# Moving a sum of x from VectorE to GpSimd, with a new order for a pair's weights, taps, a gate and W_out's forms

## What is computed

```
hn   = rms_norm(x) * norm_g
h, b, c, z, a, g, zb = split(hn @ w_in)           # 1024 -> 7 x 512
out_a = b * conv3(c * h) * silu(z)
out_b = silu(layer_norm(conv31(a * sigmoid(g)) + bias)) * silu(zb)
y    = rms_norm(x + concat(out_a, out_b) @ w_out) * final_norm_g
```

## Time and profile before

| what | value |
|---|---|
| median of 3 runs | 1524.84 us (1523.97 to 1525.23) |
| the profiled execution's own time | 1527.43 us |
| its span | 1525.6 us |
| TensorE busy | 1506.6 us, 99% |
| VectorE busy | 1325.2 us, 87% |
| GpSimd busy | 658.0 us, 43% |
| ScalarE busy | 588.8 us, 39% |

### The profile page before, as it was taken

How to read it: one execution, slowest core, us unless ns; L and a number is a source line. 1 busy time by engine, 2 the same in 40 slices (tenths; PEclk the granted TensorE clock), 3 DMA queues, 4 the chain that set the end, 5 groups by cost and what they waited for, 6 DMA issues and landing times.

```text
span 1525.6 us, 19727 instructions
## 1 busy us (share of the span) xinstructions
PE 1506.6 (99%) x7114; PEld 1326.9 (87%) x7114; DVE 1325.2 (87%) x1339; ACT 588.8 (39%) x981; POOL 658.0 (43%) x569
## 2 busy tenths in 40 slices
PE   9999999999999999999999999999999999999998
PEld 8889999988888888888888888888888778888886
DVE  7899999999998899879899894798799788888875
ACT  7543342433342343333253322224444344444433
POOL 4777869312423341243432241116654444444441
PEclk9999999999999999999999999999999999999999
DMA  6798787789998889899878977766877754555541
GB/s 248 291 352 322 278 309 264 273 295 333 313 325 268 271 274 352 299 327 290 276 251 281 314 244 233 240 221 204 243 223 222 257 179 170 177 191 180 179 152 69
DMA packets 119416, 388.75 MB, mean 255 GB/s; under 512 B 17804, under 2 KB 23052, under 8 KB 115736
## 3 DMA queue, kind: packets, MB, share of 16 engines
q1 hardware_dynamic: 116776, 387.36, 74.8%
q10 hardware_dynamic: 2544, 0.14, 0.1%
HBM read 278.98 MB, written 108.47 MB: 254 GB/s over the span
## 4 chain that ended last, share of the span: by engine, by line
PE 92%; DVE 5%; issue 1%; DMA 1%; POOL 1%; ACT 0%; POOLq 0%; DVEq 0%; ACTq 0%
PE ps L2344 30%; PE ps L2346 30%; PE ps L2345 30%; DVE ps L2085 1%; PE ps L2466 0%; DMA outa_spill<-sets 0%; PE ps L2459 0%; DVE xf L1923 0%; PE ps L2479 0%; DMA conv_b<-conv_spill 0%; DVE conv_a_acc L2029 0%; PE ps L2550 0%; PE ps L2554 0%; DVE conv_b L2125 0%; DVE w_ring L1895 0%
## 5 line engine op out<-in xcount | busy, mean ns | idle before, releaser
L2085 DVE SCALAR_TENSOR_TENSOR ps<-v,conv_b_taps,ps 128x920 f32<-128x920 f32 (+2 forms) x580 | 630.6, 1087 | 17.4
L2344 PE MATMUL ps<-xf,w_ring 128*128 128x460 f32 (+1 forms) x1624 | 603.9, 372 | 4.2 <-ACT sets L1564 2.6
L2346 PE MATMUL ps<-xf,w_ring 128*128 128x460 f32 (+1 forms) x1624 | 603.3, 371 | 0.0
L2345 PE MATMUL ps<-xf,w_ring 128*128 128x460 f32 (+1 forms) x1624 | 601.5, 370 | 0.0
L2344 PEld LDWEIGHTS ps<-xf,w_ring 128*128 128x128 f32 x1624 | 305.8, 188 | 39.4 <-ACT sets L1564 3.7
L2345 PEld LDWEIGHTS ps<-xf,w_ring 128*128 128x128 f32 x1624 | 305.8, 188 | 34.0
L2346 PEld LDWEIGHTS ps<-xf,w_ring 128*128 128x128 f32 x1624 | 305.3, 188 | 34.3
L1564 ACT ACTIVATE sets<-ps 128x460 f32<-128x460 f32 x168 | 92.6, 552 | 476.7 <-PE ps L2346 457.2
L1323 POOL TENSOR_TENSOR w_ring<-w_ring_f,w_ring 128x512 fp32r<-128x512 f32 x28 | 39.8, 1422 | 217.1 <-ACT w_ring L1594 217.1
L2344 PE MATMUL ps<-out_forms,w_ring 128*128 128x512 f32 x288 | 114.6, 398 | 2.5 <-DVE h_rows_odd L2273 2.0
L2346 PE MATMUL ps<-out_forms,w_ring 128*128 128x512 f32 x288 | 112.9, 392 | 0.0
(11 more groups left out here) (231 smaller groups left out, 2137.6 us busy)
## 6 DMA issues: line engine op xcount, KB each, us to landing
w_ring<-weight_forms SPq DMA_DIRECT2D x294, 512.0 KB, 5.4
weight_forms<-xf SPq DMA_DIRECT2D x7, 2048.0 KB, 11.5
weight_forms<-w_ring SPq DMA_DIRECT2D x7, 2048.0 KB, 10.4
out_weight_forms<-w_ring SPq DMA_DIRECT2D x28, 512.0 KB, 6.7
w_ring_f<-in_w_in SPq DMA_DIRECT2D x56, 256.0 KB, 3.6
x_raw<-in_xT SPq DMA_DIRECT2D x31, 460.0 KB, 7.0
xf_f<-in_w_in SPq DMA_DIRECT2D x24, 512.0 KB, 6.9
x_row<-in_x_prompt SPq DMA_DIRECT2D x24, 512.0 KB
```

What stands on the lines that cost most here:

```text
L2085: dve.scalar_tensor_tensor(dst, window, wb[:, j, k:k + 1], part, ALU.mult, ALU.add).then_inc(taps_done, 1)
L2344: pe.matmul(out, ahi, bhi, start=(start and x == 0), stop=False, skip_group_check=goes_on)
L2345: pe.matmul(out, ahi, blo, start=False, stop=False, skip_group_check=goes_on)
L2346: mm = pe.matmul(out, alo, bhi, start=False, stop=(stop and x == len(terms) - 1), skip_group_check=goes_on)
```

## The change

`FORM_START = II + 5` begins W_out's forms in n = 19 instead of 15. `tap_quota` gives n = 2 and 3 four and six taps instead of eight and nine, and twelve instead of eleven to periods g = 5 and 9 of units 1 to 3. Pair 3's raw weights are loaded, copied and split earlier: on SyncE before `store_sums(1)`, on ScalarE before pair 0's second gate, on VectorE inside pair 0's work; for it GpSimd does `weight_sums(2)` before `sums_low(1)`. At a unit's beginning `gate_a` of the pair before comes ahead of P4's low half. And step 3 of the sums of x goes from VectorE to GpSimd, as the first instruction of the unit's first period.

```diff
 def tap_quota(n):
...
+    if n < 4:
+        return 4 if n == 2 else 6
...
-    return 11 if u < 4 else 12
+    return (12 if g in (5, 9) else 11) if u < 4 else 12
...
+FORM_START = II + 5
...
-    e, j = divmod(n - II - 1, FORM_PERIODS)
+    e, j = divmod(n - FORM_START, FORM_PERIODS)
...
             store_weights(1)
+            load_w(3)
             store_sums(1)
...
-                if n + 2 < II:
+                if 3 < n + 2 < II:
                     load_w(n + 2)
...
+            def last_form_sum(w):
+
+                pool.wait_ge(xf_sum, 4 * (w - 1) + 3)
+                pool.wait_ge(xf_lo, 7 * (w - 1) + P2 + 1)
+                pool.tensor_tensor(st[:, 1, :, :], st[:, 1, :, :], st[:, 0, :, :], ALU.subtract).then_inc(xf_sum, 1)
...
+            weight_sums(2)
             sums_low(1)
-            weight_sums(2)
...
             for n in range(II, III):
+                if n % G14 == 0:
+                    last_form_sum(unit(n))
                 if n > II:
                     last_quarter(n - 1)
...
             weight_high(2, 3)
+            weight_high(3, 0)
+            weight_high(3, 1)
             evacuate(0, 2)
...
-                else:
+                elif n > 2:
                     weight_high(n + 1, 0)
                     weight_high(n + 1, 1)
...
-                else:
-                    dve.wait_ge(xf_lo, 7 * (w - 1) + P2 + 1)
-                    dve.tensor_tensor(st[:, 1, :, :], st[:, 1, :, :], st[:, 0, :, :],
-                                      ALU.subtract).then_inc(xf_sum, 1)
...
                         scale_tile(1, 3)
+                        weights_low(3)
                     first_tile_made(n, "B")
...
-                if n < II - 1:
+                if 2 < n < II - 1:
                     weights_low(n + 1)
...
                     form_low(unit(n), P7)
-                    form_sum(unit(n), 3)
                     form_low(unit(n), P3)
+                    finish(n - 1)
                     form_low(unit(n), P4)
-                    finish(n - 1)
```

More of the change, by code:

```diff
@@ L1910, in form_sum @@
                                       ALU.subtract).then_inc(xf_sum, 1)
-                elif step == 2:
+                else:
                     dve.wait_ge(xf_lo, 7 * (w - 1) + P1 + 1)
                     dve.tensor_tensor(st[:, 0, :, :], st[:, 2, :, :], st[:, 0, :, :], ALU.add).then_inc(xf_sum, 1)
-                else:
-                    dve.wait_ge(xf_lo, 7 * (w - 1) + P2 + 1)
-                    dve.tensor_tensor(st[:, 1, :, :], st[:, 1, :, :], st[:, 0, :, :],
-                                      ALU.subtract).then_inc(xf_sum, 1)
             def form_low(w, i):
```

## The result

The changed kernel takes 1532.41 us (median of 8 executions, 1530.84 to 1534.53); the kernel before, run beside it, 1524.86. The ratio is 1.0045, 95% interval 1.0031 to 1.0059: slower by 7 us (7.5 by the medians), as predicted (1532.8). The profiled execution took 1534.53 us, its span 1532.7; the span before was 1525.6.

A forecast was written before the change was run, and what follows sets the result against it. TensorE, busy 99% of the span, was taken as the bound, with VectorE able to be late at units' beginnings. Units' beginnings +9.3 and unit 0 -1.3 gave +8.0 us on 1524.84: 1532.8 us, range 1518 to 1536.

The forecast's parts named there:

- GpSimd's long sum: Units' first periods: P4's sum as one 1840-column GpSimd instruction takes 4.1 us and holds VectorE's low half; net +9.3 us.
- The rival without a hold: Units' beginnings: GpSimd's long sum does not hold VectorE up and the 5.2 us go; 1518.3 us, chance 0.20.
- The order by turns: Units' beginnings: VectorE and GpSimd instructions of SBUF operands alternate, each for its whole length; the waiting one is next.
- the rival at 1523.4: Units' beginnings: sum holds VectorE, but form step and last quarters slip behind P4's low half; pair 3's weights in time; chance 0.15.
- VectorE instructions which read PSUM are not touched: Units' beginnings: VectorE work reading PSUM runs beside GpSimd unhindered; a GpSimd step takes 1.19 us beside it.
- the heading: "P4's sum on GpSimd", units' beginnings: moving the sum off VectorE makes low halves late; losses 14.5 us, net +9.3.
- Waits at the units' beginnings: TensorE late: unit 1 P3 0.25, P4 1.8 us; unit 2 P4 3.0; unit 3 P7 0.6, P3 0.7, P4 3.0.
- Slow stretches: Units 1 to 3: 1.7 us more lost to a slower clock behind each late P4.
- The 5.2 us now lost: Units 2 and 3: present losses of 0.7, 0.96, 1.9 and 1.7 us go, as gate_a is earlier and spills have landed.
- Unit 0: Pair 3's earlier weights and seven taps fewer bring `v` 1.3 us earlier; bounds 0 and 5.3 us.
- the wait and its slow stretch stay: Unit 0: TensorE's wait for pair 3's `v` and the slow clock behind it remain, though `v` comes 1.3 us earlier.
- The third rival: Unit 0: pair 1's store lands at 66 or later, unit 0 loses 2 us, rest stays; 1536 us, chance 0.10.

The follow-up runs named there:

- e2: Kernel before with only the sum of P4's x moved to GpSimd, gate_a still behind P4's low half: 1525.82 us, ratio 0.9997.
- e5: Changed kernel with gate_a put back behind P4's low half, the sum staying on GpSimd: 1525.53 us, ratio 0.9994.
- e1: Changed kernel with the sum of P4's x back on VectorE, gate_a staying ahead of P4's low half: 1527.03 us, ratio 1.0009.
- e10: Changed kernel with the sum back on VectorE and gate_a back behind P4's low half: 1528.72 us, ratio 1.0015.
- e8: Kernel before with only gate_a moved ahead of P4's low half, the sum staying on VectorE: 1529.20 us, ratio 1.0018.
- e6: Kernel before with two parts only, the sum on GpSimd and gate_a ahead of P4's low half: 1536.87 us, ratio 1.0066.
- e7: Changed kernel with GpSimd's sum put behind its last quarter and gate product in the unit's first period: 1527.64 us, ratio 1.0009.
- e9: e5's kernel with four taps of n = 4, 5 and 6 cut to 8 columns, leaving work out: 1521.68 us, ratio 0.9971.
- e4: Kernel before with only unit 0's parts, pair 3's weights earlier and the taps changed: 1526.22 us, ratio 1.0000.
- e3: Changed kernel with GpSimd's sum in four instructions of 460 columns instead of one of 1840: 1537.19 us, ratio 1.0078.

## Why the prediction came out right, and where its steps were off

**GpSimd's long sum: right.** 4.18 us in unit 2 against 4.13 from the line through two rows, and it holds VectorE's low half for its whole length. The rival without a hold (1518.3) falls by the timelines above, and the hold shows in e2 and e5 too. The order by turns came out instruction by instruction, the form step ahead of P4's low half included, on which the rival at 1523.4 turned: P4's low half ends at +17.5, I had +18.0. The Trainium skill (SBUF — State Buffer, "Who interferes with whom") says that a VectorE instruction with two SBUF inputs contends with a GpSimd instruction that reads SBUF, and that the lock is exclusive. The timelines of unit 2 agree, as the low half waits through all that is left of the 4.18 us; who is next shows in the timelines alone: each time the one that waited. That VectorE instructions which read PSUM are not touched was read from a row that shows it for half a microsecond only (VectorE goes on to a low half at 543.91); after the change three of them (544.62, 545.16 and 545.71) run beside the sum and take 0.62 us each, as before.

**What the loss hangs on: half said.** My working had gate_a wait for GpSimd's product "ahead of P4's low half", but as one step among several; the heading gave the price to the sum. e2, e5 and e1 against e10 show no cost of either move alone, and e8 2.7 us (0.6 to 5.0) of the 10.1 that both cost in e6. I could have seen it: without gate_a and the form step in between, my own times put P4's low half of unit 2 at 15.6, close to due.

**Waits at the units' beginnings: right in sum.** Predicted 2.05 in unit 1, 3.0 in unit 2 and 4.3 in unit 3, 9.35 together; found 3.12, 2.55 and 3.49, 9.16. In unit 1 P2's low half ends at +4.0, not at the +2.3 of my working: the two low halves take 4.06 us, as I had it, but begin 0.9 us later (292.24), and the period begins 0.8 us earlier. So P3 is late too (1.18 us).

**Slow stretches: the mis-sized term.** I counted one of 1.7 us behind each late P4, 5.1. Only the wait of 2.40 us in unit 2 had one, 1.55 us. The waits of 1.31 and 2.39 had none. That is 3.5 of the 4.2 us by which the units' beginnings were too large in my sum.

**The 5.2 us now lost: gone**, for the reasons given: gate_a ends 1.9 and 1.3 us earlier in the periods of units 2 and 3, and TensorE comes so late to the next pair that its spill has landed. e10 shows the other side of it, with P4 in time and 4.56 us of waiting behind it.

**Unit 0: -1.2 for -1.3, and luck in it.** The steps hold: pair 1's store had landed by 62.6 (62.8 predicted), the gate stood at 65.94 (65 or later), pair 4's low halves began at 89.12 (88.1), and `v` came 1.9 us earlier instead of 1.3. What I had wrong: "the wait and its slow stretch stay". The wait for `v` fell to 1.34 us, with no slow stretch, so that up to n = 4 unit 0 gained 3.8 us. Then it gave 2.6 back in n = 7, at pair 6's gate_b (168.04). VectorE has only 0.2 to 0.6 us of idle time in each period from n = 4 to 13, while the taps taken out of n = 2 and 3 leave it idle there (5.9 us in n = 3, 0.3 before). Its load alone does not make the wait, though: e7 has the same unit 0, arrives as early, and does not wait in n = 7. The same instructions run shorter there: from 107 us on, gate_b's start is 4.9 us nearer. Two of them after the change, with GpSimd's low halves beside them, then the two and gate_b in e7:
```profile
149.60 2.83 DVE L2037 TENSOR_SCALAR conv_a_acc<-u,conv_a_taps 128x910 f32<-128x910 f32 x1
152.47 5.34 DVE L2040 SCALAR_TENSOR_TENSOR conv_a_acc<-u,conv_a_taps,conv_a_acc 128x910 f32<-128x910 f32 x2
```
```profile
148.68 6.02 POOL L1210 TENSOR_TENSOR w_ring<-w_ring_f,w_ring 128x1024 fp32r<-128x1024 f32 x2
```
```profile
146.71 1.72 DVE L2037 TENSOR_SCALAR conv_a_acc<-u,conv_a_taps 128x910 f32<-128x910 f32 x1
148.46 4.20 DVE L2040 SCALAR_TENSOR_TENSOR conv_a_acc<-u,conv_a_taps,conv_a_acc 128x910 f32<-128x910 f32 x2
...
162.89 0.58 DVE L2052 TENSOR_TENSOR conv_a_acc<-ps,conv_a_acc 128x416 f32<-128x416 f32 x1
```
I read the difference as waits inside VectorE's instructions for operands that GpSimd has; no run here takes GpSimd's work away to show it. The wait of n = 7 then comes from VectorE's work and these waits together, and how the two engines fall against each other differs from profile to profile. In e9 the first of the two is short as well (1.72), so the 3.9 us there are not four taps alone. The seven profiles with the new unit 0 and all their taps lose 3.3 to 7.2 us in n = 2 to 13, the four with the old one 6.5 to 7.7: that this one gave -1.2 shows no more than that the size was not far off, and e4, 1.0000 in time, can't tell it from nothing.

**Not foreseen:** 2.3 us on transfers of weights in n = 45 and 46, which landed after 14.1 and 12.7 us, and 0.6 in n = 0. The transfers' waits were in this profile and in e8's, in no other; what n = 0 loses lies between 0.2 and 1.9 us from profile to profile. So the 0.4 us between prediction and result are no measure of how well I knew the parts: 4.2 too much at the units' beginnings and 2.9 too little elsewhere nearly cancel, and the profiled execution lies 2.1 us above the median.

**The third rival** (the store at 66 or later) falls by 62.6.

## What to carry to other kernels

When two moves use the same slack, price them together: alone the sum cost nothing that shows, and gate_a's move 2.7 us in one surrounding and nothing in the other; together they cost 8 us more than that. Where an instruction is moved ahead of one that is due, follow what it waits for on the other engine, and what a second move has just queued ahead of that. And where the engine that feeds TensorE has no idle time in a stretch, an earlier start there can be lost again; whether that is its work or waits inside its instructions, compare the durations of equal instructions.

## What the runs showed that I had not expected

- Cutting a GpSimd instruction into four made the whole slower: 4.18 us became 8.27, because VectorE takes a turn between the pieces, and what is queued behind on GpSimd pays (e3).
- The same waiting time can cost more in few long waits than in many short ones. In the changed kernel 9.2 us of waits at the units' beginnings, in pieces up to 2.40, came with one slow stretch; in e3 11.0 us in three pieces came with three (16.9 us lost there against 10.7). The length of a wait does not settle it: one of 1.93 us had a slow stretch before the change, those of 2.32 and 2.39 after it and of 2.47 in e8 had none, and the wait of 3.32 us for `v` had one before the change and none in e6.
- The spill issued in n = 42 landed 6.1 us after its issue in e5's profile, 7.0 in that of the kernel before, 8.6 and 8.7 in the changed kernel's and e1's, 10.2 in e10's: enough to hide what a schedule change of 1.8 us gives.
